# Trailing sums left undivided, sample products and K/V low parts on GpSimd, more PSUM banks for the group norm, cached keys loaded earlier

## The reference, cut to what matters

```python
h = x @ w_in + b_in
a, g, p = jnp.split(h, [D_CONV, 2 * D_CONV], axis=-1)          # 512 channels each
u = a * jax.nn.sigmoid(g)
# head A: causal depthwise convolution, width 31, over u; then per-token group norm
y = conv(concat([ctx, u])) + conv_b
y = silu((y - mu) * lax.rsqrt(var + LN_EPS) * gn_g + gn_b)     # 8 groups of 64 channels
# head B: trailing mean over 2, 4, 8 or 16 positions minus the token, then a 128x128 map
delta = win_sum / count - p
mixed = einsum("btgc,gcd->btgd", delta, pool_w) * pool_scale
x = LN1(alpha * x + concat([silu_conv, mixed]) @ w_out)
x = LN2(alpha * x + CrossAttn(x, K, V))   # 4 heads x 256, 256 memory tokens;
                                          # the samples use cached K and V, 16 MB
x = LN3(alpha * x + relu(x @ w1 + b1)**2 @ w2 + b2)
```

## Time and profile before

| | us |
|---|---|
| median of 3 runs (1453.9 to 1457.93) | 1454.04 |
| profiled execution, its own time | 1453.77 |
| profiled execution, span of the trace | 1451.9 |
| PE busy | 1374.4 (95%) |
| DVE busy | 780.2 (54%) |
| POOL busy | 671.3 (46%) |
| ACT busy | 346.3 (24%) |

### The profile page before, as it was taken

The page is one execution under the profiler, slowest core; times in us unless marked ns, Lnnn a source line. Parts: engine busy times, 40 slices in busy tenths (PEclk is TensorE's granted clock), DMA queues, the critical chain, the costliest instruction groups (busy, mean ns, idle before and its releaser), DMA issues.

```text
span 1451.9 us, 20585 instructions
## 1 busy us (share of the span) xinstructions
PE 1374.4 (95%) x8454; PEld 1317.0 (91%) x8454; DVE 780.2 (54%) x848; ACT 346.3 (24%) x659; POOL 671.3 (46%) x392
## 2 busy tenths in 40 slices
PE   7999889997899979999999999999999999999994
PEld 6999877696699968889999999999999999999993
DVE  4899998379712652477773115531154311454568
ACT  4222441212711431135320002200022100221114
POOL 3377986136752704539533333333333333343470
PEclk9999999998999989999999999999999999999997
DMA  8222432001011066301111111111111111111103
GB/s 249 61 48 80 120 131 73 15 29 30 15 44 44 6 230 231 129 17 37 37 44 55 47 44 44 43 44 43 45 53 48 44 44 43 44 44 45 43 15 119
DMA packets 44382, 93.52 MB, mean 64 GB/s; under 512 B 20256, under 2 KB 26656, under 8 KB 41888
## 3 DMA queue, kind: packets, MB, share of 16 engines
q1 hardware_dynamic: 34560, 89.73, 19.5%
q10 hardware_dynamic: 9760, 2.93, 0.8%
HBM read 85.39 MB, written 7.25 MB: 64 GB/s over the span
## 4 chain that ended last, share of the span: by engine, by line
PE 70%; DVE 19%; POOL 6%; issue 2%; ACT 2%; DMA 1%; SPq 0%; DVEq 0%; ACTq 0%; POOLq 0%
PE bank L589 22%; PE bank L590 21%; PE bank L591 21%; DVE conv_sum L1474 10%; POOL x_low L504 1%; DVE conv_sum L1483 1%; DVE x_full L1619 1%; ACT x_full L1270 1%; POOL x_full L349 1%; POOL w_low L340 1%; PE conv_sum L751 1%; DVE bank L1629 1%; DVE x_low L1461 1%; DMA dec_kv<-dec_kv_in 1%; DVE x_full L1636 1%
## 5 line engine op out<-in xcount | busy, mean ns | idle before, releaser
L589 PE MATMUL bank<-x_high,w_high 128*128 128x384 f32 (+1 forms) x1200 | 391.6, 326 | 15.2 <-POOL w_low L340 11.8
L338 POOL TENSOR_TENSOR w_high<-w_raw,ones 128x1024 fp32r<-128x1024 f32 x84 | 163.0, 1940 | 514.8 <-PE bank L591 255.3
L590 PE MATMUL bank<-x_low,w_high 128*128 128x384 f32 (+1 forms) x1200 | 388.6, 324 | 0.0
L591 PE MATMUL bank<-x_high,w_low 128*128 128x384 f32 (+1 forms) x1200 | 387.9, 323 | 0.0
L589 PE MATMUL bank<-mix,w_high 128*128 128x384 f32 (+1 forms) x1024 | 335.9, 328 | 7.3 <-DVE x_full L1726 2.8
L590 PE MATMUL bank<-mix,w_high 128*128 128x384 f32 (+1 forms) x1024 | 335.0, 327 | 0.0
L591 PE MATMUL bank<-mix,w_low 128*128 128x384 f32 (+1 forms) x1024 | 332.1, 324 | 0.0
L589 PEld LDWEIGHTS bank<-x_high,w_high 128*128 128x128 f32 x1200 | 226.1, 188 | 18.4 <-POOL w_low L340 11.2
L591 PEld LDWEIGHTS bank<-x_high,w_low 128*128 128x128 f32 x1200 | 226.4, 189 | 0.0
L590 PEld LDWEIGHTS bank<-x_low,w_high 128*128 128x128 f32 x1200 | 226.3, 189 | 0.0
L340 POOL TENSOR_TENSOR w_low<-w_raw,w_high 128x1024 fp32r<-128x1024 f32 x84 | 211.7, 2520 | 6.6
(11 more groups left out here) (244 smaller groups left out, 1687.7 us busy)
## 6 DMA issues: line engine op xcount, KB each, us to landing
w_raw<-slabs_in SPq DMA_DIRECT2D x110, 512.0 KB, 3.5
dec_kv<-dec_kv_in SPq DMA_DIRECT2D x16, 1024.0 KB, 5.4
scratch<-slabs_in SPq DMA_DIRECT2D x8, 512.0 KB, 3.6
yT_res<-x_full SPq DMA_DIRECT2D x4, 768.0 KB, 3.5
x_full<-xT_in SPq DMA_DIRECT2D x4, 384.0 KB, 5.1
x_full<-xT_in SPq DMA_DIRECT2D x2, 768.0 KB, 8.9
x_full<-xT_in SPq DMA_DIRECT2D x2, 576.0 KB, 10.9
yT_res<-x_full SPq DMA_DIRECT2D x2, 576.0 KB, 3.0
```

The costliest lines, as they stand in the source:

```text
L338: pool.tensor_tensor(high[:, slot, :], raw[:, p, :], one, ALU.mult).then_inc(high_done, 1)
L589: pe.matmul(out, w_high, x_high, start=first, stop=False)
L590: pe.matmul(out, w_high, x_low, start=False, stop=False)
L591: return pe.matmul(out, w_low, x_high, start=False, stop=last)
```

## The change

It has five parts.

- `window_mean` no longer multiplies the window's sum by 1/w (two POOL instructions for each of four groups). The sum stays undivided, ACT multiplies the tokens by w instead (`scale_tokens`, in place, behind the first `widen` of the group, with a new wait in `window_mean`), and POOL divides the four columns of `pool_scale` by w once.
- The products of `sample_conv` are made by POOL ahead of time (`sample_products`): for each block two copies of the bias and four products into spare space of `mix_full`; DVE keeps two reduces of 512 elements. The first two calls stand between the input projection's weight parts, the third in front of `gated(3)` and the low part of slab 13, the fourth in front of the low parts of the last four V slabs. `gated(3)` moves ahead of slab 13's low part and is cut in two. The four `mix_low` move ten taps later, with the last behind the whole convolution, and the first four `e1_join` move behind them.
- `kl` and `vl`, the low parts of K and V, go from DVE (behind `e1_join(7)`) to POOL (in front of the split of slab 31).
- `gn_means` and `gn_centre` go through eight banks (6, 7, 0 to 5), `gn_spread` and its multiplications through five (6, 7, 3, 4, 5). E1's stage is cut into four for the counts of banks, and its order is the same.
- SP issues the first two blocks of cached keys before the loads of slabs 46 and 47, not behind them.

```diff
+GM_BANKS, GT_BANKS = (6, 7, 0, 1, 2, 3, 4, 5), (6, 7, 3, 4, 5)
@@ SP
-        loads(S_E1 + 2, S_XO + 4)
+        loads(S_E1 + 2, S_XO + 2)
         sp.wait_ge(sem("x_restored"), 2 * NB)
         for n in range(2):
             load_dec(n, 0)
+        loads(S_XO + 2, S_XO + 4)
@@ POOL
+        def sample_products(i):
+            pool.wait_ge(sem("conv_state_in"), 16 * CB)
+            pool.wait_ge(sem("u_done"), 2 * (i + 1))
...
+            w = col("conv_w", TAPS * i, TAPS).unsqueeze(1).broadcast_to([P, SB, TAPS])
+            for h in range(2):
+                part = sample_part(i, h)
+                own.done(pool.tensor_copy(part[:, :, :, TAPS:TAPS + 1].rearrange("p t b n -> p (t b n)"),
+                                          col("conv_b", i).broadcast_to([P, 2 * SB])))
+                for t in range(2):
+                    own.done(pool.tensor_tensor(part[:, t, :, 0:TAPS], conv_dec(i)[:, :, 2 * h + t:2 * h + t + TAPS], w, ALU.mult))
+            own.wait()
+            pool.sem_inc(sem("sample_products"), 1)
@@ window_mean
+            pool.wait_ge(sem("tokens_scaled"), 2 * (PB - g))
-            own.done(pool.tensor_scalar(mean, mean, 1.0 / wn, None, ALU.mult))
-            own.link(pool.tensor_scalar(mdec, mdec, 1.0 / wn, None, ALU.mult))
...
         mem_low(0, 0)
-        widen(0, 1)
         window_mean(0)
+        sample_products(2)
+        gated(3)
         mem_low(1, 0)
         mem_low(2, 0)
-        gated(3)
         mem_low(3, 0)
         with pool.Fori(1, MEM_SLABS // 4 - 1) as i:
             for k in range(4):
                 mem_low(k, i)
+        sample_products(3)
         for k in range(4):
             mem_low(k, MEM_SLABS // 4 - 1)
...
+        pool.tensor_tensor(kl[:], kf[:], kh[:].bitcast(f32), ALU.subtract).then_inc(sem("kv_low"), 1)
...
+        pool.tensor_tensor(vl[:], vf[:], vh[:].bitcast(f32), ALU.subtract).then_inc(sem("kv_low"), 1)
         split(31, 1, 15, MEM_SLABS)
@@ PE
-                u = 3 * i + c
-                b = 6 + u % 2
-                take(b, FREED["GM"][b] + u // 2)
+                turn, b = divmod(3 * i + c, 8)
+                b = GM_BANKS[b]
+                take(b, FREED["GM"][b] + turn)
@@ ACT
+        def scale_tokens(g):
+            act.wait_ge(sem("tokens_read"), PB - g)
+            for tokens in (qf[:, CB + g, PCTX:PEXT], pool_dec(g)[:, :, PCTX:DPEXT]):
+                act.activation(tokens, tokens, ACT.Copy, scale=float(WINDOWS[g])).then_inc(sem("tokens_scaled"), 1)
@@ DVE
-            for t in range(ST):
-                tmp = conv_sum[:, t * n:(t + 1) * n].rearrange("p (b n) -> p b n", b=SB)
-                own.done(tt(tmp, conv_dec(i)[:, :, t:t + TAPS], w, ALU.mult))
...
+            for h in range(2):
+                ins = dve.tensor_reduce(out[:, 2 * h:2 * h + 2], sample_part(i, h), AX, ALU.add)
...
-        conv(CB - 1, 0, 14)
+        conv(CB - 1, 0, 24)
         mix_low(0)
-        conv(CB - 1, 14, 17)
+        conv(CB - 1, 24, 27)
         mix_low(1)
-        conv(CB - 1, 17, 20)
+        conv(CB - 1, 27, 30)
         mix_low(2)
-        conv(CB - 1, 20, 22)
+        conv(CB - 1, 30)
         mix_low(3)
-        conv(CB - 1, 22, 25)
-        e1_join(0)
-        conv(CB - 1, 25, 29)
-        e1_join(1)
-        conv(CB - 1, 29)
-        e1_join(2)
-        e1_join(3)
+        for j in range(4):
+            e1_join(j)
```

More of the change, by code:

```diff
@@ L84 @@
 HALVES = (times(4, SIX), (5,))
+GM_BANKS, GT_BANKS = (6, 7, 0, 1, 2, 3, 4, 5), (6, 7, 3, 4, 5)
+E1_STAGE = (("E1", 0), ("E1", 1), ("E1B", 0))
 STAGES = [("IN", times(6, SIX), (2, 5)), ("K", *ONE_BANK), ("V", {0: 1, 1: 1, 3: 1, 4: 1}, (3, 4)),
-          ("PM", {b: 3 for b in POOL_BANKS}, ()), ("E1", *HALVES), ("GM", {6: 6, 7: 6}, ()), ("GV", {6: 1}, ()), ("GT", {6: 6, 7: 6}, ()),
+          ("PM", {b: 3 for b in POOL_BANKS}, ()), ("E1", times(2, SIX), (5,)), ("GM", {b: GM_BANKS[:4].count(b) + 1 for b in range(8)}, ()),
+          ("E1B", SIX, (5,)), ("GV", {6: 1}, ()), ("E1C", {0: 1, 1: 1, 2: 1}, ()),
+          ("GT", {b: [GT_BANKS[u % 5] for u in range(12)].count(b) for b in GT_BANKS}, ()), ("E1D", {3: 1, 4: 1, 5: 1}, (5,)),
           ("E2", *HALVES), ("C1", LN_MEAN, ()), ("T1", SIX, ()),
@@ L446, in _ @@
         low(4)
+        for g, wn in enumerate(WINDOWS):
+            pool.tensor_scalar(col("pool_scale", g), col("pool_scale", g), 1.0 / wn, None, ALU.mult).then_inc(sem("scale_set"), 1)
+        pool.wait_ge(sem("scale_set"), PB)
+        sample_products(0)
         low(5)
@@ L449, in _ @@
         low(6)
+        sample_products(1)
         widen(3, 1)
@@ L463, in _ @@
         window_mean(2)
-        low(11)
         widen(1, 1)
         widen(1, 2)
+        low(11)
+        widen(0, 1)
         window_mean(1)
         mem_low(0, 0)
-        widen(0, 1)
         window_mean(0)
+        sample_products(2)
+        gated(3)
         mem_low(1, 0)
         mem_low(2, 0)
-        gated(3)
         mem_low(3, 0)
@@ L486, in _ @@
             restore(b)
+        pool.wait_ge(sem("k_out"), 16)
+        pool.tensor_tensor(kl[:], kf[:], kh[:].bitcast(f32), ALU.subtract).then_inc(sem("kv_low"), 1)
+        pool.wait_ge(sem("v_out"), 16)
+        for b in (0, 1, 3, 4):
+            pool.wait_ge(free[b], FREED["V"][b] + 1)
+        pool.tensor_tensor(vl[:], vf[:], vh[:].bitcast(f32), ALU.subtract).then_inc(sem("kv_low"), 1)
         split(31, 1, 15, MEM_SLABS)
@@ L766, in _ @@
             gn_spread(i)
-        half_slab("E1", S_E1 + 3, 1, 3, CB, blocks=(1,))
+        half_slab("E1D", S_E1 + 3, 1, 0, CB, blocks=(1,))
         def ln_pivot(n):
@@ L1142, in _ @@
         pool_outputs(2)
+        scale_tokens(3)
         value(2)
@@ L1146, in _ @@
         in_high(9)
+        scale_tokens(2)
         conv_outputs(2)
@@ L1153, in _ @@
         pool_outputs(0)
+        scale_tokens(1)
         value(3)
         slab_high(S_K)
+        scale_tokens(0)
         gate(3)
@@ L1558, in _ @@
             for c, (a, z) in enumerate(CHUNKS):
-                u = 3 * i + c
-                b = 6 + u % 2
-                dve.wait_ge(full[b], FILLED["GT"][b] + u // 2 + 1)
+                turn, b = divmod(3 * i + c, 5)
+                b = GT_BANKS[b]
+                dve.wait_ge(full[b], FILLED["GT"][b] + turn + 1)
                 tt(qf[:, i, a:z], qf[:, i, a:z], ps[b][:, 0:z - a], ALU.mult).then_inc(free[b], 1)
-            for u in (3 * i + 1, 3 * i + 2):
-                dve.wait_ge(free[6 + u % 2], FREED["GT"][6 + u % 2] + u // 2 + 1)
+            for u in range(3 * i, 3 * i + 3):
+                turn, b = divmod(u, 5)
+                b = GT_BANKS[b]
+                dve.wait_ge(free[b], FREED["GT"][b] + turn + 1)
             dve.sem_inc(sem("gn_n"), 1)
@@ L1569, in _ @@
         e1_join(7)
-        dve.wait_ge(sem("k_out"), 16)
-        tt(kl[:], kf[:], kh[:].bitcast(f32), ALU.subtract).then_inc(sem("kv_low"), 1)
-        dve.wait_ge(sem("v_out"), 16)
-        for b in (0, 1, 3, 4):
-            dve.wait_ge(free[b], FREED["V"][b] + 1)
-        tt(vl[:], vf[:], vh[:].bitcast(f32), ALU.subtract).then_inc(sem("kv_low"), 1)
         def ln_block(n, scr, j):
@@ L1985 @@
         cols.append(np.asarray(v[0]).reshape(-1, P).T)
-    ramp = np.array([[1.0 / min(t + 1, w) for t in range(16)] for w in WINDOWS], np.float32).reshape(1, -1)
+    ramp = np.array([[w / min(t + 1, w) for t in range(16)] for w in WINDOWS], np.float32).reshape(1, -1)
     fixed = [np.repeat(ramp, P, 0), np.full((P, 1), EPS, np.float32),
```

59 lines of the change are left out of this document (35 added, 24 removed).

## The result

The changed kernel takes 1437.92 us (median of 4 runs, 1437.61 to 1439.9) beside 1455.99 for the kernel before on the same chip: ratio 0.9879, 95% interval 0.9857 to 0.99. The profiled execution took 1438.1 us (span 1436.3), so 15.7 less than that of before, where 22.7 were forecast. The time lies outside the forecast's own range (1427.5 to 1434.5) and inside the wide one (1422 to 1441); it is the number of the first rival.

The account below looks back on a forecast made before the run. It took PE's product lines (64% of the chain) as the bound, and the convolution while PE waits. Gains of 13.8 us up to the attention and 8.9 for keys, 22.7 off 1453.77, gave 1431.1; own range 1427.5 to 1434.5, wide 1422 to 1441.

Parts of the forecast that it names:

- first rival: Group norm: clock or bank hand-over eats the banks' gain, `gn_spread` 4.8 and products behind it 1.9 lost: 1438, chance 0.13.
- signs that it had named for being wrong: Reduces over 1 us, GpSimd products over 1.3, PE at 0.50 in group norm, or PE waiting for softmax instead of keys.
- a reduce at 0.69: Each 512-element sample reduce left on DVE takes 0.69 us, with bounds of 0.41 and 2.69.
- a product on GpSimd at 0.67: Each 248-element sample product moved to GpSimd takes 0.67 us, one call with two copies 3.1.
- the lows of K and V at nothing: Moving both subtractions from DVE to GpSimd, 10.3 us there, costs PE nothing and brings nothing on DVE.
- slab 31 split in time: Slab 31's split on GpSimd ends at about 258.4, ahead of PE's need at 267.2, with 9 us to spare.
- the wait at the sixth product: PE's wait of 1.33 us for cached keys at the sixth product stays, its load issued only when its buffer is free.
- 13.5 us of DVE work bring PE nothing here: Up to the output projection: DVE work saved goes into finishing the convolution; PE starts at 216.9 for 217.09.
- `gn_means`, 7.1 us: Group norm means: no idle time and eight banks end them by 248.3 instead of 255.4, 7.1 us gone.
- `gn_spread`, 4.8 us: Group norm multipliers: five banks bring the step from 12.17 to 7.4 us, a gain of 4.8.
- The 108 products, 1.9: Products behind `gn_spread`: if the clock does not fall, 17.9 us for 19.8, a gain of 1.9.
- Cached keys, 8.9 us: Attention: earlier key loads remove the 6.74 us wait and 2.9 of slow products, less 0.7 for softmax: 8.9 us.

Follow-up runs that it names:

- experiment 7: Changed kernel with the low parts of K and V back on DVE behind the eighth join: 1436.14 us, ratio 0.9873.
- experiment 9: Changed kernel with two banks for both group norm steps and the old order of loads, leaving only the moved DVE and GpSimd work: 1448.83 us, ratio 0.9958.
- experiment 5: Kernel before with only the banks of the change, eight for the means and five for the multipliers: 1453.59 us, ratio 0.9987.
- experiment 1: Changed kernel with two banks again for the group norm means and the multipliers: 1438.16 us, ratio 0.9882.
- experiment 2: Changed kernel with the old order of loads, all four slabs before the cached keys: 1446.14 us, ratio 0.9942.
- experiment 10: Changed kernel with two banks for both group norm steps and multiplier products over 128 rows: 1433.84 us, ratio 0.9851.
- experiment 3: Changed kernel with multiplier products contracting over 128 rows, zero-padded, instead of 24: 1432.49 us, ratio 0.9836.
- experiment 12: Kernel of experiment 8 with two banks for means and multipliers: 1426.84 us, ratio 0.981.
- experiment 8: Changed kernel plus 128-row multipliers, earlier low parts, later fourth sample products, reordered mixing banks and other last two means banks: 1423.6 us, ratio 0.9788.
- experiment 6: Kernel before with only the new order of loads, cached keys ahead of the last two slabs: 1443.83 us, ratio 0.9923.
- experiment 11: Kernel before with only the multiplier products over 128 rows, still two banks: 1447.66 us, ratio 0.9949.
- experiment 4: Changed kernel with the four mixed low parts earlier among the convolution's taps and the last sample sums behind the fourth: 1437.49 us, ratio 0.9878.

## Why the prediction was right, and where not

The direction was right, and so was the wide range; the forecast's own range missed by 3.4 us. One of the signs that it had named for being wrong came true: PE fell to 0.50 in the group norm. Terms that held: a reduce at 0.69 (0.64 to 0.69), a product on GpSimd at 0.67 (0.69), the lows of K and V at nothing (experiment 7), slab 31 split in time, the wait at the sixth product still there (1.43 us for 1.33). The sum was 22.7 us against 15.7. Step by step:

- *"13.5 us of DVE work bring PE nothing here"* holds for the start of the projection (0.8 us earlier). For the change it is the wrong credit. The moved work let the sample sums end early, and that removed PE's 3.36 idle us and the half clock behind them: with two banks in both kernels the step from the first mean to slab 30 went from 11.20 to 8.60 us, with no stretch at 0.50 left. With 0.9 us at the start, and 1.55 lost to the dip at 218, this makes 5.3 us up to the layer norm in the profiles (before and experiment 9), and 6.3 by the medians. The banks alone gave 1.6 us (experiment 5); in the changed kernel the medians give them 0.2 (experiment 1), 2.7 (experiments 9 and 2), 1.4 (10 and 3) and 3.2 (12 and 8). At one clock the profiles of 10 and 3 have 2.0. The forecast had both in one term of 7.1 and explained the shorter means by the banks. What it should have read is the half clock in the first means, which is in the earlier trace rows and which more banks could not take away: in experiment 5 PE has eight banks, doesn't wait, and runs at 0.50 for 5.8 us. Half of that is 2.9 us, and the step took 10.92 us for 8.24, 2.7 more. In experiment 6, with two banks, the clock came back after some 3.3 us, and the step took 10.20 for 8.60, 1.6 more. DVE is late in the kernel before as well, just ahead of the last of the earlier trace rows:

```profile
242.79 1.04 DVE L1488 TENSOR_SCALAR mix_full<-small,params 128x32 f32<-128x32 f32 x1
243.75 2.67 DVE L1521 SCALAR_TENSOR_TENSOR x_full<-x_full,bank 128x384 f32<-128x384 f32 x6
246.34 1.24 DVE L1530 TENSOR_TENSOR mix_full<-mix_full,conv_sum 128x384 f32<-128x384 f32 x2
```

  The sums end, then two joins run, and only then the centring begins, 2.5 us behind PE's first mean. But between 244 and 249 us PE idles only 0.12 us. The late sums are what cost: PE stood idle for them and came out of it at half the clock. The late centring by itself cost next to nothing.
- *`gn_means`, 7.1 us*: up to slab 30 the profile has 5.8. The dip at 218 us took 1.55, and the wait for bank 0 ended 8.2 us after the step began, where I had 7.6; the projection's earlier start gave 0.6 back.
- *`gn_spread`, 4.8 us*: 2.5. *The 108 products, 1.9*: nothing (20.0 us for 19.8; the 5.95 us for 36 that the term rests on are 5.92 by the rows, and at full clock the 108 took 17.6). Together 4.4 us too many, more than half of the error of 7.0. The first rival had priced this place at 6.7. That its total of 1438 came out is partly luck: the other 2.6 us come from the dip at 218, the wait for bank 0 and the keys, none of which it names. It had the right effect and the wrong cause. It blamed pacing through the banks, with a page of the Trainium skill, TensorE: Matmul & The Clock Gate, A second HAM failure mode: psum-queue depth-cycling. The page tells of PE idling briefly between groups; the prediction said that the row of 283.9 to 297.2 agrees, but that row has PE busy for 13.30 of its 13.30 us, so it shows the low clock and not the idling. With two banks and 128 rows PE is paced in the same way and the clock stays at 1.00 (experiments 10 to 12); with five banks and 24 rows it falls. What differs is the rows.
- *Cached keys, 8.9 us*: by medians 8.2 and 11.4 (experiments 2 and 6), in the profile pair 7.7. There the sixth wait was followed by slow products, 1.91 us for the 16 with keys where it had been 1.07, and 3.85 for 3.13 for the 24 behind them.
- *The product on GpSimd.* The GPSIMD Engine Reference of the Trainium skill, 4.1 Engine selection, puts GpSimd at about half of VectorE's speed with two inputs. The prediction set the average of 0.86 us on DVE against that, and it is an average over products that mostly ran beside a busy GpSimd. The second block's four ran while GpSimd stood idle:

```profile
129.17 1.41 DVE L1483 TENSOR_TENSOR conv_sum<-mix_full,params 128x248 f32<-128x248 f32 x4
```

  The four took 1.41 us together, and the shortest single one 0.41. Against that the 0.69 us on GpSimd is 1.7 times as long, which is near the page's factor; the fourth block's four took 8.77 us on DVE beside a working GpSimd. The price of 0.67 was right, and the reason given against the page was not.

The chain of medians is before 1455.2, experiment 9 1448.8, experiment 2 1446.1, changed kernel 1437.9: 6.3 us for the work on DVE and GpSimd, 2.7 for the banks, 8.2 for the keys. These add up by construction, and each is uncertain by 2 to 3 us. By the same cut the forecast's terms are 0.2 to 3.6 for DVE (with or without the 3.36 us), 10.2 to 13.6 for the banks with the clock, and 8.9 for the keys: the keys are right and the first two the wrong way round.

Open is why the clock dips at 218 us in some executions: in the profiles of the changed kernel and of experiments 4, 7, 9 and 10, not in those of 1, 2 and 3, whose code is the same up to there. The traces narrow it. All eight have the wait of 1.94 us for the low parts of a V slab at 190.8, which is new, and in 1, 2 and 3 (and in 4 as well) the clock fell right behind that wait. Experiment 1:

```profile
192.00:194.00 2.00, 2.00 (x9) 0.50 0.41 88
```

The changed kernel and experiments 7, 9 and 10 have 1.00 in this stretch. At 192 us a dip cost nothing, because PE then waits for `mix_low(0)` in any case (1.30 us at 199.8 in the changed kernel, 0.17 us or no wait in experiments 1 to 3). So every trace with the wait at 190.8 has a dip in one of the two places. None of the others has one there: the four traces with the DVE order of before, and experiments 8 and 12, where the wait is gone. (Of those four, experiment 6 alone has a dip at 158 to 162 us, behind a wait of 2.4 us for a low part that all four have.) Moving the fourth sample products alone, which would take only that wait away, wasn't tried, so that the wait causes the dip is not shown.

## What to carry to other kernels

When a step is slow, look first at what its start waited for and at the granted clock behind that wait, and only then at how many buffers lie between. Two banks were enough for the means once PE came to them without standing idle, and eight did little while it stood idle first. Where a small contraction runs for several microseconds, try it padded to all 128 rows with zeros in the stationary matrix (what lies in the other rows of the moving operand must be finite): it cost PE no time here (the first four instructions took 1.45 us with 128 rows and 1.55 with 24) and was worth 4 to 8 us. And split a forecast so that each term names one edit; a term that two edits share can't be wrong in a way that teaches.

## What the hardware showed

Products that contract over 24 rows let the granted clock fall to 0.50 (1.2 GHz) though PE is busy without a gap: in all nine traces with 24 rows it fell 3 to 6 us after the first multiplier and stayed there for 10 us and more, in none of the five with 128 rows. The variances, which contract over 128 rows and write 24, kept 1.00 in every trace. TensorE: Matmul & The Clock Gate of the Trainium skill, What's actually happening, says that the clock follows how busy PE has been; PE's busy time alone does not explain these rows, since it is the same in both versions.

After 3.36 us without work PE ran at 0.50 for 3 to 6 us in all four traces that have this wait (before, experiments 5, 6 and 11), and how long differed between executions of the same code: 5.6 us in the kernel before and 3.3 in experiment 6, whose code is the same there.
